# Feature-major projections in two halves of 320 tokens instead of 512 and 128

## The chip, the core and the metric

One core of one Trainium2 chip runs the kernel. The metric is the time on the device of one execution in microseconds; it is given as the median of several runs.

## What is computed

One step of a small diffusion trunk with two layers, on two groups of tokens: 512 latent tokens (x_sample, conditioned by c) and 128 context tokens (x_prompt, conditioned by c_ctx). All arithmetic is f32. Cut to what matters:

```python
D_MODEL = 1024; SEQ = 128; DEC_SEQ = 512; DEPTH = 2
H_A = H_B = H_C = 4        # three branches of 4 heads, 512 features each
N_EXPERTS = 16; D_EXPERT = 1024

h = rmsnorm(x, g_norm1) * (1.0 + sc1) + sh1          # sc1, sh1: by token group
(qa, ka, va, qb, kb, vb, zb, ab, bb, qc, kc, vc, ga, gb, gc) = split_cols(h @ w_in)
oa = diff_attention(rope(qa), rope(ka), va, ...)     # softmax(q1 k1) - lam * softmax(q2 k2)
ob = gated_head_norm(bidir_gated_delta(conv_silu(qb, kb, vb), ...), zb)
oc = neighborhood_attention(qc, kc, vc, k_ctx, v_ctx, rpb)
merged = sum(sigmoid(g_i) * (o_i @ w_br_i))
x += gate1 * (merged @ w_out)
x += gate2 * expert_choice_ffn(adaLN(rmsnorm(x)))    # 16 experts
```

Rotary positions are applied to the 512 latent tokens of qa and ka alone.

## The kernel before

**Layout.** Activations are kept feature-major: hT holds 8 groups of 128 features on the partitions and all T = 640 tokens as columns, 512 latent and then 128 context tokens. A feature-major projection (kind "fm": qb, kb, vb, zb, qa, ka, kc, qc, the gates ga and gb) loads a chunk of 1024 x 512 weights into one of three ring slots and makes 512 features, in four tiles of 128, from 8 matmuls each. "br" (w_br, 512 inputs, 4 matmuls a tile), "wo" (w_out) and "late" (the gate gc) have the same form. "tm" (va, vc) is token-major: the tokens are the weights, five units of 512 columns.

**Units.** A projection is 5 units. The first makes the 128 context columns of all four tiles into the four quarters of one PSUM bank; the others make the 512 latent columns of one tile each. Units alternate between two PSUM banks (ps). `begin(n)` lets TensorE start unit n when ScalarE has copied out unit n-2 (`unit_emptied`); `used` signals `unit_computed`.

**Order of a layer.** Program order is written out by hand on each engine.
1. Norm: VectorE scales, ScalarE shifts hT group by group (`h_ready`, L1398); TensorE's first project (L735 to L751) waits for each group k.
2. qb, kb, vb, zb by `project` (L743 context, L749 latent); ScalarE copies to `pre` (padded), VectorE convolves.
3. DeltaNet: eight L2 norms, five turns of k and v, ten groups of 128 tokens (GROUPS) of 15 dependent steps each, four output turns. After each step TensorE takes a number of quanta from a list: GAPS[gap], with STEPS = (5, 3, 2, ..., 2, 4) within a group, 5 in ("l2", j), 2 in ("kv", t), 4 in ("o", h). The list FILL holds the eight later ada chunks and folds and va, qa, kc, ka, qc, vc and the gates ga, gb. A quantum of `fill_rows` is one matmul of 512 columns (L801) or four of 128 (L792), one of `fill_tokens` (L813) is one matmul of 512. What is left of the list when the gaps are over is done before attention. ScalarE copies each unit at the gap in which it ends (DRAINS, `drain`) to one of NSTAGE = 8 stage slots of 512 columns, which lie where x was (x is spilled to memory). SP stores them (`store_plan`), waiting first for the slot of the next weight chunk (`load_plan`). The slot of unit n is used again by unit n+8.
4. Rotation: the 8 latent units of qa and ka are rotated on VectorE at hooks behind steps 7, 8, 10 and 14 of the groups, up to three of four operations a hook (a shuffle and three tensor_tensor, L1871 to L1877). GpSimd stores them one after the other (L663, `rotated_stored`).
5. Two attentions (17 query units each: one of context, then four heads of four latent tiles). SP loads K and Q when the last state is updated (L536). TensorE's loop of a unit i: scores(i+2), weigh of the finished head, late quanta, turn(i) (L1110), each of which waits for the softmax of ScalarE and VectorE. `late_units` (L829, L832) has 40 quanta: 8 at i = 0, 4 at each second and third tile of a head. ScalarE copies a late unit (L1609) behind the probabilities of the third tile.
6. Branches b, c, a, two halves each: `project` with 4 matmuls a tile; ScalarE copies a unit to `brs` (two buffers) or `brsp` (context), takes the gate's sigmoid behind the first copy (L1644), and VectorE multiplies and adds into `merged` (L2083 to L2086). After the first half-branch TensorE sums squares of oa (`sub_sums`, L1158); ScalarE takes five square roots behind the third unit of the second (L1652, L1653); VectorE scales oa head by head (`scale_sub`, L2074 reciprocal, L2075) behind four merges, SUB_AT = [(0, 1, 2), (1, 0, 0), (1, 0, 2), (1, 1, 0)] (branch, half, tile). Branch a waits for all four (`sub_scaled`).
7. wo (L1175, L1182): ScalarE scales a unit with gate1, VectorE adds it to x, then ScalarE squares and VectorE sums a feature group for the next norm.
8. The expert layer, whose 96 chunks of 2 MB a layer are loaded by SP all along.

Of the kernel before, what the change touches and what calls it, by code (L numbers as in the profile page):

```python
# [24 lines left out]
ALU = mybir.AluOpType  # L25
# [9 lines left out]
NT = T // P  # L35
NTS = TS // P
# [26 lines left out]
UNITS_OF = dict(ada=1, fm=5, tm=5, br=5, late=0)  # L63
# [44 lines left out]
XADDS = 12 + KD  # L108
# [47 lines left out]
def chunk_used(c):  # L156

    l, q = c // LAYER_CHUNKS, c % LAYER_CHUNKS
    if q < PRE_CHUNKS:
        name, i = PLAN[q]  # L160
        if kind_of(name) == "late":
            return "late_computed", 5 * (2 * l + i + 1)
        return "unit_computed", unit_no(l, name, i) + UNITS_OF[kind_of(name)]
# [47 lines left out]
NSTAGE = 8  # L211
STEPS = (5, 3, 2, 2, 2, 2, 2, 2, 2, 2, 2, 2, 2, 2, 4)
GAPS = {("l2", _j): 5 for _j in range(8)}
GAPS |= {("kv", _t): 2 for _t in range(5)}
GAPS |= {(_i, _j): _q for _i in range(10) for _j, _q in enumerate(STEPS)}
GAPS |= {("o", _h): 4 for _h in (4, 0, 1, 2, 3)}


def fill_units():

    units = []
    for name, i in FILL:
# [4 lines left out]
        else:  # L227
            units += [(name, i, j, 8) for j in range(5)]
# [23 lines left out]
ROTATED = [(_n, _j) for _n in ("qa", "ka") for _j in range(1, 5)]  # L252
# [3 lines left out]
def rotations():  # L256
# [16 lines left out]
def stage_no(name, i, j):  # L273
    return 5 * SPILLED.index((name, i)) + j
# [9 lines left out]

STAGED = [plain_stores(_d, 5 * len(SPILLED) - 1) for _d in range(NSTAGE)]


def stored(l, n):
# [3 lines left out]
    return f"stage{n % NSTAGE}_stored", 16 * (l * STAGED[n % NSTAGE] + plain_stores(n % NSTAGE, n))  # L292

# [41 lines left out]
def build(nc, A, O):  # L335
    with ExitStack() as ctx:
# [55 lines left out]
        stage = [xflat[:, 512 * i:512 * i + 512] for i in range(NSTAGE)]  # L392
        adarow = [at(7680, (512,)), xflat[:, 512 * NSTAGE:512 * NSTAGE + 512]]
# [16 lines left out]
        rot = xflat[:, 512 * (NSTAGE + 1):512 * (NSTAGE + 1) + TS]  # L410
# [4 lines left out]
        lstage = [[xflat[:, 512 * j:512 * j + 512] for j in range(5)], [at(10240 + 512 * j, (512,)) for j in range(5)]]  # L415
        gsig = [xflat[:, 0:4 * T].rearrange("p (k t) -> p k t", k=4)] + [at((17408, 12800)[i % 2], (4, T)) for i in range(5)]
        brs, brsp = at(15360, (2, TS)), at(16384, (H, TP))
        xtmp, xtmpp = at(0, (2, TS)), at(2 * TS, (H, TP))
# [34 lines left out]
        def tile_t(t):  # L453
            return slice(t * P, (t + 1) * P)

# [21 lines left out]
        def _(sp):  # L477
# [14 lines left out]
            for l in range(DEPTH):  # L492
# [15 lines left out]
                def store_plan(q):  # L508
# [4 lines left out]
                    for j in range(5):  # L513
                        n = stage_no(name, i, j)
                        if n in ROTATED_AT:
                            continue
                        sp.wait_ge(sig["unit_emptied"], unit_no(l, name, i, j) + 1)
                        if kind_of(name) == "tm":
                            dst = to[:, 512 * j:512 * j + 512]
                        elif j:  # L520
# [1696 lines left out]
```

## Time and profile before

| | us |
|---|---|
| median of 3 runs | 3558.13 (3557.75 to 3559.14) |
| the profiled execution | 3554.68 |
| its span, first to last instruction | 3552.9 |
| TensorE matmuls busy | 3376.7 (95%) |
| VectorE, ScalarE busy | 1218.2 (34%), 785.6 (22%) |

The profile has a page (shares of busy time, the span in 40 slices, DMA queues, the chain of work that ended last, groups of instructions) and a trace that is asked in views. An f32 matmul shows as two records. A record's duration is longer than the distance to the next one, because matmuls are pipelined; how fast TensorE goes is read from the distance between starts, which the chain of work adds up ("64 records, 27.47 us"). A bracket at a timeline row is the idle time ahead of it and what ended it. The clock column is TensorE's granted clock as a share of 2.4 GHz, 0.5 is 1.2 GHz. Layer 0 runs from 50 to 1750 us, layer 1 from there on.

### The profile page before, as it was taken

To read this page: it belongs to the slowest core of one execution; us is meant where nothing else is said; L and a number is where in the kernel's file an instruction comes from. 1 tells how busy PE (TensorE), PEld (TensorE's weight loads), DVE (VectorE), ACT (ScalarE), POOL (GpSimd) and SP (SyncE) were. 2 spreads that over 40 slices of the span, in tenths; PEclk is the share of its full clock that TensorE was granted. 3 is DMA by queue.
4 is the path that set the end of the run, shared out by engine and by line. 5 is a ranking of instruction groups with operands and counts; after the bars stand their busy time and mean duration, and the time that the engine had idled before them with its cause. 6 is when DMAs were issued, how large, how long until landed. Compare 5 with 4: busy or idle time off the path is not lost.

```text
span 3552.9 us, 47524 instructions
## 1 busy us (share of the span) xinstructions
PE 3376.7 (95%) x20823; PEld 1891.9 (53%) x20823; DVE 1218.2 (34%) x2250; ACT 785.6 (22%) x1695; POOL 151.9 (4%) x179
## 2 busy tenths in 40 slices
PE   7999999999999699999989999999999987999997
PEld 4557767765555244443455577677655543444444
DVE  3454443347452400000143644343563532000003
ACT  3131111125332211111122211111343321111112
POOL 1000000000100000000100000000000000000000
PEclk9999999999999899999999999999999998999999
DMA  7342332341342599999932433241532417999994
GB/s 220 98 122 72 94 93 71 94 136 60 110 162 72 204 381 393 389 395 386 369 114 71 111 88 94 67 123 39 175 98 89 153 51 285 395 389 389 394 390 163
DMA packets 217935, 675.15 MB, mean 190 GB/s; under 512 B 9786, under 2 KB 22312, under 8 KB 214144
## 3 DMA queue, kind: packets, MB, share of 16 engines
q1 hardware_dynamic: 197376, 611.35, 48.8%
q0 software_dynamic: 14640, 47.78, 5.0%
q10 hardware_dynamic: 5712, 12.99, 0.9%
q8 instruction: 164, 2.69, 0.3%
q14 instruction: 43, 0.35, 0.0%
HBM read 610.63 MB, written 66.68 MB: 191 GB/s over the span
## 4 chain that ended last, share of the span: by engine, by line
PE 90%; DVE 3%; DMA 3%; ACT 3%; issue 1%; ACTq 0%; DVEq 0%
PE unit L1257 12%; PE unit L801 12%; PE unit L749 11%; PE work L1260 9%; PE work L1257 6%; PE unit L813 4%; PE unit L792 3%; PE unit L1182 3%; PE unit L832 3%; PE unit L743 3%; PE unit L1131 2%; PE work L996 2%; PE work L1030 2%; PE unit L759 1%; PE work L1096 1%; DMA ring<-in_w_e_gate 1%
## 5 line engine op out<-in xcount | busy, mean ns | idle before, releaser
L801 PE MATMUL unit<-hT,ring 128*128 128x512 f32 x1024 | 475.5, 593 | 0.0
L1257 PE MATMUL unit<-ring,arena 128*64 128x512 f32 x1568 | 357.3, 601 | 4.3 <-DMA ring<-in_w_e_gate 2.1
L1260 PE MATMUL work<-ring,arena 128*32 128x256 f32 x4608 | 274.8, 382 | 0.0
L801 PEld LDWEIGHTS unit<-hT,ring 128*128 128x128 f32 x1024 | 177.9, 191 | 140.6 <-issue 140.6
L2167 DVE TENSOR_SCALAR arena<-work,arena 64x512 f32<-64x512 f32 x32 | 24.1, 755 | 662.5 <-PE work L1257 662.5
L1257 PEld LDWEIGHTS unit<-ring,arena 128*64 128x64 f32 x1568 | 110.7, 138 | 225.8 <-issue 219.9
L1260 PEld LDWEIGHTS work<-ring,arena 128*32 128x32 f32 x4608 | 136.8, 109 | 159.8 <-issue 80.8
L749 PE MATMUL unit<-hT,ring 128*128 128x512 f32 x512 | 221.1, 592 | 0.0
L1257 PE MATMUL work<-ring,arena 128*64 128x512 f32 x736 | 166.5, 594 | 2.1 <-ACT arena L1713 2.1
L749 PE MATMUL unit<-arena,ring 128*128 128x512 f32 x384 | 166.8, 592 | 0.0
L749 PEld LDWEIGHTS unit<-hT,ring 128*128 128x128 f32 x512 | 96.7, 190 | 118.6 <-issue 118.6
L1353 ACT ACTIVATE xT<-unit 128x512 f32<-128x512 f32 x108 | 64.4, 596 | 428.7 <-PE unit L801 318.5
L813 PE MATMUL unit<-ring,hT 128*128 128x512 f32 x320 | 146.7, 594 | 0.0
L2157 DVE TENSOR_TENSOR arena<-unit,arena 128x512 f32<-128x512 f32 x32 | 22.1, 692 | 353.9 <-PE unit L1257 353.9
L792 PE MATMUL unit<-hT,ring 128*128 128x128 f32 x1024 | 125.1, 276 | 0.0
L792 PEld LDWEIGHTS unit<-hT,ring 128*128 128x128 f32 x1024 | 119.1, 192 | 6.9 <-issue 6.9
L749 PEld LDWEIGHTS unit<-arena,ring 128*128 128x128 f32 x384 | 72.1, 190 | 86.1 <-issue 86.1
L832 PE MATMUL unit<-hT,ring 128*128 128x512 f32 x256 | 116.5, 598 | 0.0
L1182 PE MATMUL unit<-arena,ring 128*128 128x512 f32 x256 | 110.5, 592 | 0.0
L1353 ACT ACTIVATE arena<-unit 128x512 f32<-128x512 f32 x80 | 47.7, 597 | 280.7 <-PE unit L749 280.7
L1257 PE MATMUL unit<-arena 128*64 128x512 f32 x480 | 109.6, 598 | 0.0
L1257 PEld LDWEIGHTS work<-ring,arena 128*64 128x64 f32 x736 | 51.8, 137 | 103.9 <-issue 103.0
(415 smaller groups left out, 4743.6 us busy)
## 6 DMA issues: line engine op xcount, KB each, us to landing
ring<-in_w_e_gate SPq DMA_DIRECT2D x50, 2048.0 KB, 13.8
ring<-in_w_e_up SPq DMA_DIRECT2D x48, 2048.0 KB, 13.6
ring<-in_w_e_down SPq DMA_DIRECT2D x46, 2048.0 KB, 15.0
ring<-in_w_in SPq DMA_DIRECT2D x32, 2048.0 KB, 15.3
ring<-in_w_ada SPq DMA_DIRECT2D x24, 2048.0 KB, 8.9
arena<-in_w_e_down SPq DMA_DIRECT2D x18, 2048.0 KB, 14.6
arena<-in_w_e_up SPq DMA_DIRECT2D x16, 2048.0 KB, 13.1
arena<-in_w_e_gate SPq DMA_DIRECT2D x14, 2048.0 KB, 15.3
```

The lines of the kernel that those rows point to most:

```text
L743: last = mm(bank[:, tile_t(m)], w[:, k, m * P:(m + 1) * P], src[:, k, TS:T], start=k == 0, stop=k == kk - 1)
L749: last = mm(bank[:, :], w[:, k, m * P:(m + 1) * P], src[:, k, 0:TS], start=k == 0, stop=k == kk - 1)
L792: last = mm(bank[:, tile_t(m)], w[:, k, m * P:(m + 1) * P], hT[:, k, TS:T], start=k == 0, stop=k == KD - 1)
L801: last = mm(bank[:, :], w[:, k, m * P:(m + 1) * P], hT[:, k, 0:TS], start=k == 0, stop=k == KD - 1)
L813: last = mm(big[:, :], hT[:, k, tile_t(t)], w[:, k, :], start=k == 0, stop=k == KD - 1)
L832: last = mm(ps[1][:, :], w[:, s, (j - 1) * P:j * P], hT[:, s, 0:TS], start=s == 0, stop=s == KD - 1)
L996: last = mm(W[(3, 1, 3)[s]][:, tile_t(h)], gD4[:, h, :], (gX if s else gP)[:, h, :], start=True, stop=True)
L1030: last = mm(W[(1, 0, 1)[s]][:, tile_t(h)], gZT[:, h, :], (gV if s else gV0)[:, h, :], start=True, stop=True)
L1182: last = mm(bank[:, :], w[:, k, m * P:(m + 1) * P], merged[:, k, 0:TS], start=k == 0, stop=k == KD - 1)
L1257: last = mm(big[SLS * c:SLS * c + SLS, :], x, w[:, kk, 512 * c:512 * c + 512], start=k == 0, stop=k == KD - 1)
L1260: last = mm(low[SLOTP * c:SLOTP * c + SLOTP, 0:256], xp, w[:, kk, 256 * c:256 * c + 256], start=k == 0, stop=k == KD - 1)
L1353: emptied(a_(dst, unit(n)[:, :], f))
```

## The change

All 640 tokens of a feature-major projection are taken as two halves of HT = 320 columns, so the second half holds 192 latent and the 128 context columns. A projection is then 8 units of 320 columns (fm: tile by tile, both halves; br and wo: all tiles of the first half, then of the second). Token-major units stay at 5 of 512.

- Fill: fill_rows has 64 quanta of one matmul of 320 columns. GAPS becomes 8 for l2, 3 for kv, STEPS = (8, 5, 3, ..., 3, 6), 6 for o.
- Staging: 10 stage slots of 320 columns for fm, 2 of 512 for tm; SP stores all units but two of a chunk before it waits to load the next one, and the last two behind.
- Rotation: 16 pieces (320 or 192 columns), up to four operations a hook.
- Late: 8 units, 8 quanta at each second and third tile of a head; a copy behind the probabilities at both.
- Branches: merges in halves; gates' sigmoid behind unit 0; the square roots behind unit 3 of the second half-branch; SUB_AT applies at the second half of its tile (unit 4 + tile).
- wo: units of one tile and one half; residual and squares follow; x is added in 16 pieces.

```diff
-UNITS_OF = dict(ada=1, fm=5, tm=5, br=5, late=0)
+UNITS_OF = dict(ada=1, fm=8, tm=5, br=8, late=0)
+NLATE = 8
...
-NSTAGE = 8
-STEPS = (5, 3, 2, 2, 2, 2, 2, 2, 2, 2, 2, 2, 2, 2, 4)
-GAPS = {("l2", _j): 5 for _j in range(8)}
-GAPS |= {("kv", _t): 2 for _t in range(5)}
+NSTAGE = 10
+NROWSTAGE = 2
+STEPS = (8, 5, 3, 3, 3, 3, 3, 3, 3, 3, 3, 3, 3, 3, 6)
+GAPS = {("l2", _j): 8 for _j in range(8)}
+GAPS |= {("kv", _t): 3 for _t in range(5)}
...
-GAPS |= {("o", _h): 4 for _h in (4, 0, 1, 2, 3)}
+GAPS |= {("o", _h): 6 for _h in (4, 0, 1, 2, 3)}
...
-ROTATED = [(_n, _j) for _n in ("qa", "ka") for _j in range(1, 5)]
+ROTATED = [(_n, _j) for _n in ("qa", "ka") for _j in range(8)]
...
-        n = min(3, 4 * len(ready) - at)
+        n = min(4, 4 * len(ready) - at)
...
                 for q in range(8, last + 3):
+                    store_plan(q - 3, False)
                     load_plan(q)
-                    store_plan(q - 3)
+                    store_plan(q - 3, True)
...
             def project(l, name, i, src, kk=KD, wait=None):
-                for m in range(4):
+                for u in range(8):
+                    m, f = (u % 4, u // 4) if kind_of(name) == "br" else (u // 2, u % 2)
+                    bank = begin(unit_no(l, name, i, u))
                     for k in range(kk):
-                        if wait and m == 0:
+                        if wait and u == 0:
                             pe.wait_ge(*wait(k))
-                        last = mm(bank[:, tile_t(m)], w[:, k, m * P:(m + 1) * P], src[:, k, TS:T],
-                                  start=k == 0, stop=k == kk - 1)
-                used(last)
-                for m in range(4):
-                    bank = begin(unit_no(l, name, i, 1 + m))
-                    for k in range(kk):
-                        last = mm(bank[:, :], w[:, k, m * P:(m + 1) * P], src[:, k, 0:TS],
+                        last = mm(bank[:, 0:HT], w[:, k, m * P:(m + 1) * P], src[:, k, half_t(f)],
                                   start=k == 0, stop=k == kk - 1)
                     used(last)
...
                         if i and AUNITS[i][1] in (1, 2):
                             if AUNITS[i][1] == 1:
                                 pe.wait_ge(sig["attn_out"], NPV * nb + AUNITS[i][0] + 1)
-                            for _ in range(KD // 2):
-                                next(extra)
+                            for _ in range(KD):
+                                next(extra, None)
...
-                        if i and AUNITS[i][1] == 2:
-                            copy_late(1 + AUNITS[i][0])
+                        late = 2 * AUNITS[i][0] + AUNITS[i][1]
+                        if i and AUNITS[i][1] in (1, 2) and late < NLATE:
+                            copy_late(late)
...
+                        for u in range(8):
+                            at_ = 8 * (6 * l + g) + u
+                            if at_ >= 2:
+                                act.wait_ge(sig["merged_ready"], at_ - 1)
+                            copy_unit(unit_no(l, "br" + s, half, u), brs[:, u % 2, :], words=HT)
+                            if u == 0:
+                                act.wait_ge(sig[f"gate{half}_loaded"], 16 * (3 * l + b + 1))
+                                a_(gsig[g], gsig[g], ACT.Sigmoid).then_inc(sig["gate_ready"], 1)
+                            if g == 1 and u == 3:
...
+                            merge(merged[:, 4 * half + m, half_t(f)], gsig[2 * b + half][:, m, half_t(f)], brs[:, u % 2, :])
+                            if f and (b, half, m) in SUB_AT:
                                 scale_sub(SUB_AT.index((b, half, m)))
```

## Rows read from the trace of the kernel before

**Rows 1.** The page: busy us with share and count; the granted clock in 40 slices.
```profile
PE 3376.7 (95%) x20823; PEld 1891.9 (53%) x20823; DVE 1218.2 (34%) x2250; ACT 785.6 (22%) x1695; POOL 151.9 (4%) x179
PEclk9999999999999899999999999999999998999999
```

**Rows 2.** Stretches: length; busy of PE, PEld, DVE, ACT, POOL; clock; DMA; GB/s.
```profile
300.00:600.00 300.00, 300.00 (x1741) 212.37 (x1740) 130.84 (x256) 47.99 (x110) 3.77 (x7) 1.00 0.35 92
...
975.00:1155.00 180.00, 178.90 (x661) 99.63 (x660) 65.33 (x75) 54.15 (x73) 0.00 (x0) 1.00 0.32 116
```

**Rows 3.** The chain of work that ended last: start, length, records.
```profile
59.21 27.47 PE unit L749 x64
86.68 7.14 PE unit L743 x64
```

**Rows 4.** Timeline, TensorE, matmuls of two columns: start, length.
```profile
34.89 1.05 PE L770 MATMUL work<-cst,arena 128*128 128x2 f32 x8
```

**Rows 5.** Grouped view, 128-column records: first and last of five: busy, mean ns, idle.
```profile
L792 PE MATMUL unit<-hT,ring 128*128 128x128 f32 x1024 | 125.1, 276 | 0.0
...
L1175 PE MATMUL unit<-arena,ring 128*128 128x128 f32 x256 | 29.2, 275 | 0.0
```

**Rows 6.** Timeline, TensorE and VectorE, end of the DeltaNet stage, layer 0.
```profile
763.37 1.88 PE L801 MATMUL unit<-hT,ring 128*128 128x512 f32 x4
...
769.48 7.03 PE L801 MATMUL unit<-hT,ring 128*128 128x512 f32 x16
779.09 0.65 PE L1053 MATMUL work<-cst,arena 128*128 128x128 f32 x4 [2.57 <-DVE arena L1962]
...
769.68 1.12 DVE L1946 SCALAR_TENSOR_TENSOR arena<-arena,sc,work 128x128 f32<-128x128 f32 x4 [2.82 <-PE work L1042]
...
775.93 3.10 DVE L1962 TENSOR_TENSOR arena<-arena,sc 128x512 f32<-128x512 f32 x5
...
791.23 0.63 PE L1068 MATMUL work<-cst,arena 128*128 128x128 f32 x4 [1.15 <-ACT xT L1353]
```

**Rows 7.** Timeline, TensorE, last head of the first attention, layer 0.
```profile
875.11 3.60 PE L832 MATMUL unit<-hT,ring 128*128 128x512 f32 x8
...
880.22 0.66 PE L1110 MATMUL unit<-cst,arena 128*128 128x128 f32 x4 [1.08 <-DVE arena L2053]
```

**Rows 8.** Branch stage: timeline of ScalarE and VectorE, then groups for the widths.
```profile
1008.90 1.28 ACT L1652 ACT_TABLE_LOAD   x1
1010.20 2.42 ACT L1652 ACTIVATE arena<-work,cst 128x512 f32<-128x512 f32 x4
...
1042.28 4.15 DVE L2074 RECIPROCAL arena<-arena 128x640 f32<-128x640 f32 x1
1046.46 0.89 DVE L2075 SCALAR_TENSOR_TENSOR arena<-arena,vcol 128x640 f32<-128x640 f32 x1
...
L2158 DVE TENSOR_TENSOR arena<-work,arena 128x256 f32<-128x256 f32 x32 | 13.3, 414 | 0.0
...
L2086 DVE TENSOR_TENSOR arena<-arena 128x512 f32<-128x512 f32 x40 | 27.7, 692 | 1.4
...
L1713 ACT ACTIVATE arena<-work 128x256 f32<-128x256 f32 x32 | 12.1, 379 | 0.0
...
L1353 ACT ACTIVATE arena<-unit 128x512 f32<-128x512 f32 x80 | 47.7, 597 | 280.7 <-PE unit L749 280.7
```

**Rows 9.** Stretches behind two lulls of TensorE, columns as in rows 2.
```profile
200.00:204.00 4.00, 4.00 (x16) 1.08 (x18) 1.38 (x1) 1.92 (x3) 0.00 (x0) 0.50 0.03 11
...
1795.00:1800.00 5.00, 3.40 (x9) 2.25 (x10) 5.00 (x11) 5.00 (x11) 0.00 (x0) 0.50 0.15 50
```

**Rows 10.** TensorE's waits (total, times, longest), and the chain at layer 1's start.
```profile
PE unit L743 <- ACT hT L1398: 7.1, 1, 7.1
...
1794.99 7.50 ACT hT L1398 x16
```

**Rows 11.** GpSimd's stores of the rotated units (L663), from issue to landing.
```profile
DMA to landing us min/median/max: 2.3/2.3/11.7
```

More of the change, by code:

```diff
@@ L227, in fill_units @@
         else:
-            units += [(name, i, j, 8) for j in range(5)]
+            units += [(name, i, j, KD) for j in range(UNITS_OF[kind_of(name)])]
     return units
@@ L282, in plain_stores, with row_stores @@
     return sum(n not in ROTATED_AT for n in range(d, last + 1, NSTAGE))
-STAGED = [plain_stores(_d, 5 * len(SPILLED) - 1) for _d in range(NSTAGE)]
+def row_stores(d, last):
+    return len(range(d, last + 1, NROWSTAGE))
+STAGED = [plain_stores(_d, 8 * len(COL_SPILLED) - 1) for _d in range(NSTAGE)]
+ROWSTAGED = [row_stores(_d, 5 * len(ROW_SPILLED) - 1) for _d in range(NROWSTAGE)]
 def stored(l, n):
@@ L391, in build @@
         xflat = xT.rearrange("p k t -> p (k t)")
-        stage = [xflat[:, 512 * i:512 * i + 512] for i in range(NSTAGE)]
-        adarow = [at(7680, (512,)), xflat[:, 512 * NSTAGE:512 * NSTAGE + 512]]
+        stage = [xflat[:, HT * i:HT * i + HT] for i in range(NSTAGE)]
+        rowstage = [xflat[:, HT * NSTAGE + 512 * i:HT * NSTAGE + 512 * i + 512] for i in range(NROWSTAGE)]
+        behind = HT * NSTAGE + 512 * NROWSTAGE
+        adarow = [at(7680, (512,)), xflat[:, behind:behind + 512]]
         (gE, gL, gAT, gD, gDT, gI, gD2, gD2T, gD4, gP, gX, c32, gN, gVB, gKB, gKD) = [
@@ L533, in spilled @@
                     sp.wait_ge(sig["rotated_stored"], 16 * (l * len(ROTATED) + r))
+                    last = 5 * sum(f in ROW_SPILLED for f in before) - 1
+                    for d in range(NROWSTAGE):
+                        sp.wait_ge(sig[f"rowstage{d}_stored"], 16 * (l * ROWSTAGED[d] + row_stores(d, last)))
                 def back(dst, name, i, done):
@@ L818, in late_units @@
             def late_units(l, i):
-                for j in range(5):
-                    n = 5 * (2 * l + i) + j
+                for j in range(NLATE):
+                    n = NLATE * (2 * l + i) + j
                     w = chunk_in(chunk_no(l, *LATE[i]))
@@ L1350, in copy_context, with copy_unit @@
                 emptied(a_(dst, h4(unit(n)), f))
[L1352 to L1353 removed]
+            def copy_unit(n, dst, f=ACT.Copy, words=512):
+                emptied(a_(dst, unit(n)[:, 0:words], f))
             def ada(l, a):
@@ L2107, in _ @@
                 dve.wait_ge(sig["x_moved"], 16 * (2 * l + 2))
                 for half in range(2):
-                    add_x(unit_no(l, "wo", half), half)
+                    for u in range(8):
+                        m, f = u % 4, u // 4
+                        dve.wait_ge(sig["unit_emptied"], unit_no(l, "wo", half, u) + 1)
+                        x = xT[:, 4 * half + m, half_t(f)]
+                        TT(x, x, xtmp[:, u % 2, :], ALU.add).then_inc(sig["x_added"], 1)
+                        if f:
+                            add_square(2 * l + 1, 4 * half + m)
```

231 lines of the change are left out of this document (102 added, 129 removed).

## The prediction

> **What bounds the kernel now.** I read the page's shares and clock first: TensorE is busy 3376.7 of 3552.9 us at nearly the full clock, so it is the bound unless a stage says otherwise [rows 1]. The table of stretches says where: in the DeltaNet stage (300 to 600 us) it is busy 300 of 300 us, and in the branch and output projections (975 to 1155) 178.9 of 180 [rows 2]. Two things therefore count: the time that TensorE's own matmuls take, and each place where the change takes away work that now covers a wait.
>
> A trace record is one pass; an f32 matmul has two. In the chain, 64 records of 512 columns take 27.47 us and 64 of 128 columns take 7.14 [rows 3]. So the **pitch** is 429.2 ns at 512 columns and 111.6 at 128. One projection unit of the kernel before (16 records) is 6.87 us, its 128-column unit (64 records) 7.14 us, and a whole projection 34.6 us.
>
> **Part 1, the halves themselves.** Each pair of a 512- and a 128-column record (540.8 ns) becomes two of 320. There are 1024+512+384+256+256 = 2432 such pairs, in five groups of the grouped view; its first and last stand in [rows 5]. No 320-column record is in the trace. Eight records of 2 columns last 1.05 us together, the last one about 0.27, so their pitch is 0.111 us too [rows 4]: at 128 columns the pitch is the weights' load, not the columns. 1024 column-cycles at 2.4 GHz are 426.7 ns, so a 512-column record has 2.5 ns on top; a 320-column one by the same account takes 266.7+2.5 = 269.2 ns. Bounds: in proportion 268.3, on the line between the two pitches 270.4. I take 269.2, since it rests on the longer record, in which the columns are the limit. 2432 x (540.8 - 538.4) = **-5.8 us** (bounds -10 and 0). The Trainium skill ("TensorE: Matmul & The Clock Gate", section on the extra 2.5 ns) gives a fixed 2.5 ns for every matmul whatever its width. That rule by itself would make the halves worth nothing, as there are as many matmuls as before; the trace's 111.6 at both 2 and 128 columns speaks for a small gain.
>
> A layer starts with TensorE waiting for hT: in layer 1 7.1 us for the first group, and then ScalarE delivers eight groups in 7.5 us, one every 0.94 [rows 10]. TensorE fills these waits with two records of 128 columns per group now and two of 320 then, so it has more done when the last group comes; the clock is at its lower level there [rows 9]. Layer 0 gains next to nothing (there most groups are ready when the weights land), layer 1 some 2.5: **-2.7 us**. The last unit's copy in front of the L2 norms and the last one of wo are shorter: 0.2 us each, twice per layer, **-0.8 us**.
>
> **Part 2, the fill of the DeltaNet stage.** Between its dependent steps TensorE takes "quanta" from a list. Before: 424 quanta for 430 slots of GAPS, so the list ends in the gap after the third output turn. After: 24 for ada and fold, 80 for va and vc, 8 x 64 = 512 for the rest, 616 in all. The slots become 64+15+550+30 = 659. va and vc keep their 512-column quanta but are now taken three at a time where two were taken, so the list runs dry early: 574 slots lie ahead of group 9, 42 quanta are left for its 55 slots, and they end in its gap 11. Empty are gaps 12, 13 and 14 of group 9 and all five "o" gaps. Everywhere else a gap of 3 x 0.538 = 1.62 us stands for 2 x 0.858 = 1.72 (four records 763.37 to 765.09) [rows 6]. VectorE's answer in such a gap takes 0.2 + 0.69 us, so some 0.7 us of slack stays and the narrower gap costs nothing.
>
> Now the end of the stage in layer 0 [rows 6]. From L1042's end at 769.48 VectorE needs until 775.93 + 3.10 = 779.03 for the normed output, 9.55 us. Before, 16 records (6.87 us) covered it and TensorE waited 2.57. After, nothing covers it: +6.9. Gaps 12 and 13 become waits of 0.9 us each: +1.8. Of the four output turns each waits for VectorE's two scalings (1.1 us), before hidden but for 1.15 us at 791.23: 0.7 + 0.4 + 1.5 after, +1.4. Together **+10.0 us a layer, +20.0**. The K and Q loads that attention needs start with the last state update, then about 13 us ahead of attention; I take them as hidden; uncovered they would add at most some 3 us a layer.
>
> **Clock.** TensorE then stands nearly idle for some 15 us. The trace has its clock at 1.2 GHz after each lull: 0.50 at 200 to 204, though busy 4.00 of 4.00, and 0.50 at 1795 to 1800 [rows 9]. So I expect the turns, the key turns and the first 3 to 6 us of attention at half speed: +3.5 us a layer, bounds 0 and +7. With a smaller lull at the end of the first attention (+1): **+9 us**.
>
> **Part 3, attention with the late projection.** Before: 40 quanta, 8 at the start and 4 in each of eight slots. After: 64, 8 at the start and 8 (4.31 us) in the first seven slots; the eighth, in the last head, is empty. The work is the same, its cover is not. The last slot holds 8 records (3.43 us) at 875.11, and TensorE still waits 1.08 us behind it for VectorE [rows 7]. In the first attention all 3.4 us turn to waiting, plus 0.4 for a copy (ScalarE, 320 columns) that now stands in front of the last exponentials: +3.9. The second has shorter exponentials, so about 1.5 of it, plus 0.25 at each second slot of a head, where TensorE now waits until ScalarE has emptied the bank: +2.6. The copies (0.43 where it was 0.60) in front of exponentials that TensorE waits for give back 0.17 seven times: -1.2. **+5.3 us a layer, +10.6** (bounds 0 and 8 a layer).
>
> **Part 4, branch projections.** Units are now 8 of 2.15 us (8 records), where they were 3.57 and four of 3.43; buffers are two in PSUM and two in SBUF either way. So TensorE may run ahead of a blocked ScalarE or VectorE by less time. Widths: VectorE 0.41 at 256 and 0.69 at 512 columns, so 0.48 at 320 and 1.0 for a merge of two operations; ScalarE 0.38 at 256 and 0.60 at 512, so 0.43 at 320 [rows 8]. I went through the units one by one with these. (a) First half-branch: the sigmoid (1.28 table + 2.34) now sits between the copies of units 0 and 1: 0.7 us. (b) The square roots for the sub-norm, 1.28 + 2.42 + 0.6 = 4.3 us on ScalarE [rows 8], now cover two units of 2.15 instead of two of 3.43: 1.1 us. (c) scale_sub is 4.15 + 0.89 = 5.0 us on VectorE [rows 8], four times; two pairs of them stand 4.3 us apart (before 6.9), each between merges of 1.0 us per 2.15. VectorE falls behind, and units 3 of half-branches 2 and 3 wait 0.4 and 2.4. (d) The fourth scale_sub comes after unit 4, at 10.8 us of its half-branch, where it came at 7.0; branch a waits for it: 0.3. Sum 4.9, **+5.0 us a layer, +10.0** (bounds 3 and 7).
>
> Staging: 8 stores instead of 5 a projection, more DMAs issued by SP, the first six ahead of the next weights' load; these loads have a whole chunk's time (34.6 us and more), so nothing. Rotation: 64 pieces instead of 32 but at 0.4 to 0.5 us instead of 0.7, about the same VectorE time per hook, with slack. wo: TensorE waits once for the first halves of the merges and once for all, each with four units of 4.31 us in hand: nothing.
>
> **Sum.** -5.8 - 2.7 - 0.8 + 20.0 + 9 + 10.6 + 10.0 = +40.3 us. The profiled execution took 3554.7 us (span 3552.9 and 1.8 around it), 3.4 below the median of the runs; 3554.7 + 40.3 + 3.4 = **3598 us**.
>
> **Rivals.**
> (A) Milder: the lull does not lower the clock long and attention's and the branches' waits are half of mine: 3598 - 9 - 10 = 3579. For it: VectorE and ScalarE are far from full over these stretches. 18%.
> (B) Staging bites: the tenth stage slot comes round after ten units of 320 columns. In group 1, kc unit 6 needs the slot of qa unit 4, rotated one hook before, and ka unit 1 that of qa unit 7. GpSimd's stores land in 2.3 us, but 11.7 when weights are under way [rows 11]. ScalarE is held in drain then, and behind it the copy for which the next merge waits. One or two such waits of 5 us a layer: 3598 + 16 = 3614. Against: the second slot is needed about 12 us after its store. 12%.
> (C) Faster: the stage is bound by the chain, not by TensorE. A record's duration exceeds its pitch (1.05 us for eight at 0.111) [rows 4], so holes below 0.16 us a gap could hide in "busy". Then the third quantum of va and vc would go into holes, and the early end of the list would cost nothing. It decides if a two-quanta gap is longer than 1.72 us. Then part 2 turns from +20 to -20 and its 7 us of clock vanish: 3598 - 47 = 3551. Against: 763.37 to 765.09 is just four pitches. 4%.
> (D) No change, the parts cancel or the late waits vanish in TensorE's slack elsewhere: 3558. 6%. By the skill's rule on width (part 1) alone the sum would be 3604; that is inside the forecast.
>
> **Chances.** Forecast (3585 to 3608) 60%, A 18, B 12, C 4, D 6. 0.2% (7 us) is about what a measurement of this kernel can tell from no change. Faster 5%, same 6%, slower 89%. The range takes in A and B, leaves out C and D and the ends: 3571 to 3616.
>
> **What would show it.** Records of 320 columns at a pitch of 269 ns; the fill's last record in gap 11 of group 9, then a wait of 9.5 us for L1962's counterpart and the clock at 1.2 GHz after it; a wait of some 4 us for the last probabilities in each layer's first attention; waits of TensorE on unit copies between 975 and 1060, the longest in the fourth half-branch. I am wrong if the fill's gaps show waits in the middle of the stage, if the pitch is off by over 2 ns, or if attention's empty slot costs nothing.

## The result, and the profile after

The changed kernel takes 3595.05 us (median of four runs, 3593.64 to 3597.39) beside 3558.07 us for the kernel before: ratio 1.0104, 95% interval 1.0088 to 1.012. It is slower by 1%, and 3598 was predicted (3571 to 3616). The medians are 37.0 us apart. The profiled execution took 3594.47 us, its span is 3592.7; between the last starts of TensorE in the two profiled executions there are 40.2 us, and the comparison by stages below goes by these.

The page answers to [rows 1]: as many matmuls, 7 us more busy, and the wait is elsewhere.

```profile
PE 3383.8 (94%) x20823; PEld 2089.6 (58%) x20823; DVE 1238.7 (34%) x2402; ACT 809.9 (23%) x1855; POOL 161.1 (4%) x195
PEclk9999999999999899999999999999999998999998
```

**The pitch.** Two rows of the chain of work that ended last (start, length, records), first a projection between two others, then wo. They answer to [rows 3].

```profile
156.04 34.66 PE unit L771 x128
...
1102.04 68.92 PE unit L1184 x256
```

256 records of 320 columns in 68.92 us are 269.2 ns each, the predicted number. (128 in 34.66 are 270.8, with the unit waits of that stretch in it.) The Trainium skill has a fixed 2.5 ns per matmul at 2.4 GHz ("TensorE: Matmul & The Clock Gate", section "Wait — 56ns, not 53.3ns?"); with the column times of part 1 the trace agrees at 320 and 512 columns: 266.7 + 2.5 and 426.7 + 2.5. At the old 128-column records the same account would be 106.7 + 2.5 = 109.2 and the trace has 111.6; these 2.4 ns a pair are the whole gain in pitch, 5.8 us over the 2432 pairs.

**The end of the fill.** TensorE's timeline in layer 0: start, length, what, records, and in brackets the idle time ahead and what ended it. It answers to [rows 6].

```profile
776.13 1.24 PE L814 MATMUL unit<-hT,ring 128*128 128x320 f32 x4
...
779.04 1.16 PE L1037 MATMUL work<-arena 128*128 128x128 f32 x8 [0.78 <-DVE arena L1949]
780.98 1.16 PE L1047 MATMUL work<-arena 128*128 128x128 f32 x8 [0.78 <-DVE arena L1949]
781.97 1.06 PE L1049 MATMUL work<-arena 128*128 128x128 f32 x8
792.47 1.11 PE L1060 MATMUL work<-cst,arena 128*128 128x128 f32 x4 [9.44 <-DVE arena L1972]
```

The last two quanta (four records) lie in gap 11 of group 9. The two gaps behind it are waits of 0.78 us, and then TensorE stands for 9.44 us where it stood 2.57. The first output turn lasts 1.11 us instead of 0.65: the clock is down.

**The clock.** Stretches of the changed kernel; columns as in rows 2, the granted clock is the last but two.

```profile
786.00:795.00 9.00, 2.50 (x11) 2.10 (x12) 4.48 (x9) 4.06 (x9) 0.00 (x0) 0.50 0.95 342
796.00:802.00 6.00, 3.45 (x35) 2.88 (x36) 3.25 (x10) 1.29 (x3) 1.21 (x3) 1.00 1.09 413
2555.00:2564.00 9.00, 4.79 (x20) 3.85 (x20) 7.09 (x14) 0.88 (x1) 0.00 (x0) 0.50 1.02 343
2564.00:2570.00 6.00, 4.67 (x28) 4.20 (x30) 1.54 (x7) 1.29 (x3) 2.80 (x4) 0.50 1.04 412
888.00:898.00 10.00, 6.99 (x14) 3.76 (x15) 2.34 (x8) 1.63 (x3) 0.00 (x0) 0.50 0.28 100
2752.00:2758.00 6.00, 5.22 (x11) 2.66 (x10) 0.00 (x0) 1.19 (x2) 0.00 (x0) 0.50 0.43 161
```

The same lull of 9.4 us stands in both layers. In layer 0 TensorE is back at 2.4 GHz when attention begins (798 us); in layer 1 it stays at 1.2 GHz for 6 us of it. The last two rows are further places: the end of the first attention in layer 0 and that of the second in layer 1.

**The end of the first attention**, layer 0, TensorE's timeline; it answers to [rows 7].

```profile
884.35 0.60 PE L1117 MATMUL unit<-cst,arena 128*128 128x128 f32 x4
885.73 0.63 PE L1117 MATMUL unit<-cst,arena 128*128 128x128 f32 x4 [0.78 <-ACT arena L1603]
890.23 1.11 PE L1117 MATMUL unit<-cst,arena 128*128 128x128 f32 x4 [3.87 <-DVE arena L2063]
...
892.97 7.09 PE L1138 MATMUL unit<-arena 128*128 128x512 f32 x10 [0.78 <-ACT arena L1606]
```

The empty slot lies between 884.35 and 885.73. The wait of 3.87 us for the last probabilities (1.08 before) is the predicted one in place and near it in size: with the wait of 0.78 ahead of it, which was not there before, 3.6 us are added, for a term of +3.9. What follows was priced at 1 us: the weigh of ten records lasts 7.09 us, where ten at full clock last 4.5, and from the start of the last turn to the weigh it is 2.74 us (890.23 to 892.97) for 1.93.

**The branch stage**, the chain in layer 0. The view keeps the longest pieces, so short ones are missing between the rows; work of DVE and ACT in the chain stands for waits of TensorE.

```profile
1020.73 1.28 ACT L1663
1022.61 1.83 ACT arena L1663 x3
1025.40 6.74 PE unit L771 x24
1032.68 1.28 ACT L1659
1034.34 1.88 issue
1036.69 4.59 PE unit L771 x16
1042.85 4.08 DVE arena L2084
1046.95 0.88 DVE arena L2085
1049.69 4.07 DVE arena L2084
1053.79 0.89 DVE arena L2085
1056.12 4.59 PE unit L771 x16
```

TensorE's starts show five waits in front of units: 0.38 us (until 996, behind the first sigmoid), 1.08 (1025, behind the roots), 0.42 (1036), 2.10 (1056, behind the second pair of scalings) and 0.32 (1067, for the last scaling). Predicted were 0.7, 1.1, 0.4, 2.4 and 0.3. The third stands where it was predicted and has the predicted size, but the chain shows another cause: not a scaling on VectorE but ScalarE's next table load (L1659, 1.28 us at 1032.68) with its sigmoid.

**The stages.** How much longer a stage takes on TensorE than before, from the first start of each stage (us; before starts at 199.10, 791.23, 887.36, 975.85 and 1153.35 in layer 0). The kernels behind "after" are those of the experiments; the changed kernel's +40.2 is the sum of its column. Each column is one execution: that of e1 was the fastest of its five (3566.87 us, median 3575.86), that of e3 the slowest of its four (3603.11, median 3597.14).

| layer, stage | after | e1 | b1 | e2 | e3 | e4 | d1 | e6 |
|---|---|---|---|---|---|---|---|---|
| 0, start to L2 norms | -2.5 | -2.7 | -0.4 | -0.8 | -0.9 | -0.7 | -1.6 | -0.5 |
| 0, DeltaNet with output turns | +9.4 | -1.0 | +9.4 | +9.7 | +9.6 | +9.8 | +9.4 | -0.9 |
| 0, first attention | +6.5 | +6.7 | +1.4 | +6.8 | +6.1 | -0.2 | +5.0 | -0.3 |
| 0, second attention | 0.0 | 0.0 | -1.7 | 0.0 | +6.7 | -1.5 | +5.7 | -1.5 |
| 0, branches and wo | +4.0 | +4.0 | 0.0 | +0.2 | +4.0 | +5.7 | +4.0 | +0.2 |
| experts of layer 0, 1 to L2 norms | -3.6 | -5.1 | +1.4 | -3.1 | -3.0 | -3.5 | -5.3 | -4.8 |
| 1, DeltaNet with output turns | +8.4 | -1.6 | +9.0 | +8.3 | +8.4 | +8.3 | +10.1 | +2.3 |
| 1, first attention | +8.8 | +6.6 | +1.6 | +8.7 | +5.7 | +1.9 | +7.7 | +1.3 |
| 1, second attention | +5.5 | +1.7 | 0.0 | +5.4 | +7.9 | +0.5 | +5.7 | +0.1 |
| 1, branches and wo | +4.1 | +4.1 | 0.0 | +0.2 | +4.1 | +4.1 | +4.1 | +0.2 |
| rest | -0.4 | 0.0 | +1.4 | -1.4 | +0.3 | +0.8 | -1.8 | -1.8 |
| all | +40.2 | +12.6 | +22.2 | +34.1 | +48.9 | +25.0 | +43.0 | -5.6 |

The sixth row mixes two things. Split at the first sum of squares of layer 1's norm (1785.78 us before), the way from there to the L2 norms is 3.9 us shorter in the changed kernel and 3.8 to 4.1 shorter in every other kernel of 320 columns, where b1 and b2, the old form, have +0.7 and +1.5. That gain is the change's own.

### The profile page after: what moved, and what is told of

Its sections match the earlier page's. It is cut to its first block, busy times and chain, and to the rows that moved or that the text cites. A ratio compares the mean times of both kernels' runs of the same rounds, so it can differ in the third digit from the quotient of the medians.

```text
span 3592.7 us, 48060 instructions
## 1 busy us (share of the span) xinstructions
PE 3383.8 (94%) x20823; PEld 2089.6 (58%) x20823; DVE 1238.7 (34%) x2402; ACT 809.9 (23%) x1855; POOL 161.1 (4%) x195
## 4 chain that ended last, share of the span: by engine, by line
PE 87%; DVE 5%; DMA 4%; ACT 3%; issue 1%; POOL 0%; ACTq 0%; DVEq 0%
PE unit L814 15%; PE unit L1259 12%; PE unit L771 12%; PE work L1262 9%; PE work L1259 6%; PE unit L826 4%; PE unit L1184 4%; PE unit L839 3%; PE unit L1138 2%; DMA ring<-in_w_e_gate 2%; PE work L1037 2%; PE work L1003 1%; PE unit L781 1%; PE work L1103 1%; PE unit L1117 1%
## 5 line engine op out<-in xcount | busy, mean ns | idle before, releaser
L814 PE MATMUL unit<-hT,ring 128*128 128x320 f32 x2048 | 600.1, 434 | 0.0
L814 PEld LDWEIGHTS unit<-hT,ring 128*128 128x128 f32 x2048 | 367.6, 191 | 126.8 <-issue 10.4
L771 PE MATMUL unit<-hT,ring 128*128 128x320 f32 x1024 | 281.0, 438 | 13.2 <-ACT hT L1400 7.2
L771 PEld LDWEIGHTS unit<-hT,ring 128*128 128x128 f32 x1024 | 197.0, 193 | 95.7 <-issue 9.6
L771 PE MATMUL unit<-arena,ring 128*128 128x320 f32 x768 | 210.3, 434 | 8.4 <-ACT arena L1355 6.7
L771 PEld LDWEIGHTS unit<-arena,ring 128*128 128x128 f32 x768 | 145.0, 190 | 73.5 <-ACT arena L1355 10.7
L1355 ACT ACTIVATE xT<-unit 128x320 f32<-128x320 f32 (+1 forms) x156 | 72.5, 465 | 435.5 <-PE unit L814 376.7
L839 PE MATMUL unit<-hT,ring 128*128 128x320 f32 x512 | 145.2, 437 | 0.1
L1184 PE MATMUL unit<-arena,ring 128*128 128x320 f32 x512 | 138.1, 432 | 0.0
L839 PEld LDWEIGHTS unit<-hT,ring 128*128 128x128 f32 x512 | 95.6, 190 | 47.0 <-issue 8.3
L1184 PEld LDWEIGHTS unit<-arena,ring 128*128 128x128 f32 x512 | 97.4, 190 | 40.4
L1355 ACT ACTIVATE arena<-unit 128x320 f32<-128x320 f32 x136 | 59.1, 437 | 271.1 <-PE unit L771 249.6
```

The costliest lines, as they stand in the source:

```text
L771: last = mm(bank[:, 0:HT], w[:, k, m * P:(m + 1) * P], src[:, k, half_t(f)], start=k == 0, stop=k == kk - 1)
L814: last = mm(bank[:, 0:HT], w[:, k, tile_t(u // 2)], hT[:, k, half_t(u % 2)], start=k == 0, stop=k == KD - 1)
L839: last = mm(ps[1][:, 0:HT], w[:, k, tile_t(j // 2)], hT[:, k, half_t(j % 2)], start=k == 0, stop=k == KD - 1)
L1184: last = mm(bank[:, 0:HT], w[:, k, m * P:(m + 1) * P], merged[:, k, half_t(f)], start=k == 0, stop=k == KD - 1)
L1355: emptied(a_(dst, unit(n)[:, 0:words], f))
```

## The experiments

The theory is that of the prediction: the halves themselves gain a little, and three places lose cover (the early end of the list, the empty late slot, blocks of 4 to 5 us on ScalarE and VectorE between short units), each with a low clock where TensorE stood. The rivals are that the 320-column form costs by itself, or that the stage is bound by its chain. Each ratio is against the kernel before as it ran beside that experiment (medians 3555.3 to 3556.0 us, where it was 3558.07 beside the changed kernel), so the difference between medians of two experiments is good to some 2 us.

### e1: the list dealt out by time

```diff
-STEPS = (8, 5, 3, 3, 3, 3, 3, 3, 3, 3, 3, 3, 3, 3, 6)
-GAPS = {("l2", _j): 8 for _j in range(8)}
...
+STEPS = (5, 3, 2, 2, 2, 2, 2, 2, 2, 2, 2, 2, 2, 2, 4)
+WIDE = {("l2", _j): 5 for _j in range(8)}
...
+        cost += dict(ada=[0.86] * 2, fold=[0.4], tm=[0.858] * 40).get(kind, [0.538] * 64)
...
+    for gap, n in WIDE.items():
+        due += 0.858 * n * SCALE
+        k = 0
+        while at < len(cost) and done + cost[at] / 2 <= due:
+            done += cost[at]
+            at += 1
+            k += 1
+        out[gap] = k
...
+SCALE = 0.985
+GAPS = gaps()
```

> The changed kernel with one thing else: the quanta of each gap of the DeltaNet stage are dealt out by time (0.538 us for a quantum of 320 columns, 0.858 for one of 512) against the time that the gap had before (5, 3, 2 ... 2, 4 quanta of 0.858 us). There are 616 slots for 616 quanta, and the last quanta lie in the last output gap. Theory (the loss is the list's early end): the wait for the normed output (L1972's counterpart) goes from 9.4 back to about 2.6 us, no stretch at 1.2 GHz between the end of the stage and the first attention in either layer, the stage with its turns 9.4 and 8.4 us shorter and layer 1's first attention some 2 more: -20 us against the changed kernel, 3575 (3570 to 3579). Rival (the stage is bound by its chain, and narrow gaps cost as much as the empty ones): 3590 to 3597, the wait short but other waits in the middle of the stage.

Measured 3575.86 us (ratio 1.0058, 1.0044 to 1.0072). The stage goes from +9.4 and +8.4 to -1.0 and -1.6 us. At its end there are matmuls of 320 columns between all output turns, and the wait for the normed output is 2.98 us ([rows 6] have 2.57):

```profile
773.19 0.66 PE L1082 MATMUL work<-cst,arena 128*128 128x128 f32 x4 [2.98 <-DVE arena L1994]
...
787.50 0.66 PE L1097 MATMUL work<-cst,arena 128*128 128x128 f32 x4 [0.59 <-ACT xT L1377]
```

So the 320-column gaps are no worse than the old ones, and 20 us of the loss (+17.8 to -2.6 in the stage) were the sizes of the gaps in a table. The first attention keeps its +6.7 and +6.6 with nothing low ahead of it: that loss is its own. In layer 1 the second attention loses 3.8 us less: here its last weigh is at full clock, where in the changed kernel the ten records take 6.72 us, and its first head is 0.9 us shorter. Why the clock fell there in the one kernel and not in the other, no run shows.

### b1: the old kernel with an early end

```diff
-GAPS = {("l2", _j): 5 for _j in range(8)}
+GAPS = {("l2", _j): 8 - (_j == 7) for _j in range(8)}
```

> The kernel before, its projections in 512 and 128, with one thing of the change alone: seven of the eight gaps of the L2 norms take 8 quanta and the last one 7, where all took 5, so that the list runs dry in gap 11 of group 9, as it does in the changed kernel. Theory: the same loss as there, 8.5 to 10 us a layer in the stage and its turns and 1 to 4 us a layer from the clock at 1.2 GHz behind it: 3558 + 22 = 3580 (3575 to 3587). Rival (the loss belongs to the 320-column form, not to the empty gaps): 3558, within 3 us.

Measured 3575.72 us (1.0057, 1.0043 to 1.0071). The old kernel now shows the same wait to the hundredth, in the place where [rows 6] have 2.57:

```profile
794.43 1.11 PE L1053 MATMUL work<-cst,arena 128*128 128x128 f32 x4 [9.44 <-DVE arena L1962]
```

+9.4 and +9.0 in the stage, and +1.4 and +1.6 in the first attention, in which nothing else was changed: the granted clock is at 0.5 for another 3.4 us from 802.2 and from 2563.4. The early end costs the same in the old form: it has nothing to do with 320 columns.

### e2: the sub-norm's work spread

```diff
-SUB_AT = [(0, 1, 2), (1, 0, 0), (1, 0, 2), (1, 1, 0)]
+SUB_AT = [(0, 1, 2), (0, 1, 4), (0, 1, 6), (1, 0, 1), (1, 0, 3), (1, 0, 6), (1, 1, 0), (1, 1, 3)]
...
-                            if g == 1 and u == 3:
+                            if g == 1 and u in (1, 2, 3, 4):
...
-                    ch.link(v_.reciprocal(rt1[:, h, :], rt1[:, h, :]))
+                    r, o = rt1[:, h, half_t(f)], oaT[:, h, half_t(f)]
+                    ch.link(v_.reciprocal(r, r))
```

> The changed kernel with the sub-norm's work spread: the square roots one head behind each of the units 1 to 4 of the second half-branch, where all stand behind unit 3, and the scaling of oa in eight pieces of 320 columns behind eight merges, where four whole heads stand behind four. The work is the same. Theory (ScalarE's 4.3 us and VectorE's 5.0 us blocks outlast the two buffers of 2.15 us units): the waits of 1.1, 0.4, 2.1 and 0.3 us in front of units go, the first one (0.4, behind the sigmoid) stays; -3.6 us a layer, -7 in all, 3588 (3586 to 3590). Rival (short units cost TensorE by their number, at every copy and merge): the stage keeps its length, 3594 to 3596.

Measured 3589.17 us (1.0094, 1.0079 to 1.011). The stage goes from +4.0 and +4.1 to +0.2 us, the theory's -3.6 to 0.3 us. In its chain the roots and the scalings are gone (two rows of layer 0):

```profile
1013.91 19.40 PE unit L771 x72
...
1037.86 62.71 PE unit L771 x232
```

Three of the four waits that were to go are gone. The one of 0.42 us stays in both layers. ScalarE's and TensorE's timelines in layer 0 name its cause, the table load and the sigmoid between the copies of two units:

```profile
1033.85 1.28 ACT L1659 ACT_TABLE_LOAD   x1
1035.14 2.34 ACT L1659 ACTIVATE arena<-arena 128x2560 f32<-128x2560 f32 x1
...
1037.86 1.34 PE L771 MATMUL unit<-arena,ring 128*128 128x320 f32 x4 [0.25 <-ACT arena L1355]
```

### e3: the empty slot at the front

```diff
-                        if i and AUNITS[i][1] in (1, 2):
+                        if i and AUNITS[i][1] in (1, 2) and i > 2:
...
-                        late = 2 * AUNITS[i][0] + AUNITS[i][1]
+                        late = 2 * AUNITS[i][0] + AUNITS[i][1] - 1
```

> The changed kernel with the empty late slot of each attention at the front: no quanta at the second tile of the first head, and units 1 to 7 one slot later each, the last one in the last head. Theory (the empty slot costs what the answer to it needs at that place, and at the end of the stage a low clock besides): at the front 4.3 us of matmuls leave a wait of 2.3, at the end 4.3 us of matmuls take the place of a wait of 3.9; with the last weigh back at full clock -4 us in each layer's first attention, and -0 to -3 in layer 1's second, where the bias of the second head comes late: 3585 (3582 to 3589). Rival (the empty slot costs the same wherever it lies): 3592 to 3596.

Measured 3597.14 us (1.0114, 1.0099 to 1.013): the theory's number is missed by 12 us. The end of the first attention does as expected (the last wait of 3.87 is 0.78, the weigh at full clock). But the front costs two waits, where one of 2.3 was expected:

```profile
816.48 0.66 PE L1117 MATMUL unit<-cst,arena 128*128 128x128 f32 x4 [2.54 <-DVE arena L2063]
...
820.51 0.66 PE L1117 MATMUL unit<-cst,arena 128*128 128x128 f32 x4 [2.09 <-DVE arena L2063]
```

and the second attention loses 6.7 and 2.4 us more. In layer 0, 4.1 of the 6.7 lie in the last head, where 4.3 us of matmuls now stand in place of a wait of 1.3. The first head is 1.5 us longer although it has 4.3 us of matmuls less, and the second 1.1. The chain names why: the bias table of the second head, behind GpSimd's five stores that clear moe_sum.

```profile
901.76 2.64 POOL moe_sum L705 x5
...
905.25 18.08 DMA arena<-rpb_scratch
```

With the front empty TensorE comes to the second head before this load has landed (no run has the empty front with the stores moved). What follows for the theory: not "a slot lost is a wait of 3.9", but a distance. From the turn of one tile to the turn of the tile after the next, ScalarE copies and exponentiates and VectorE combines, 5.9 us (884.35 to 890.23 in the fence of the changed kernel's end); a wait comes where TensorE has less than that between these two turns. The first head has a short weigh (1.2 us) ahead of its second tile, so an empty slot there is short twice.

### e4: the empty slot one place earlier in the last head

```diff
-                        if i and AUNITS[i][1] in (1, 2):
-                            if AUNITS[i][1] == 1:
+                        if i and AUNITS[i][1] in (1, 2) and i != NA - 3:
+                            if AUNITS[i][1] == 1 or i == NA - 2:
```

> The changed kernel with one late unit moved by one slot: the last unit lies at the third tile of the last head, and the second tile of that head is the empty slot. Theory (the place decides: in the records of the kernel with the empty slot at the front, TensorE's turn of a tile needs ScalarE and VectorE for some 5.6 us after the turn of two tiles before; between two such turns TensorE has its scores, a weigh or a late unit; with the second tile of a later head empty there is always one weigh or one unit of 4.3 us in between, with the third tile empty there is none): the wait of 3.9 to 4.1 us for the last probabilities goes to about 1, the weigh behind it is back at full clock, -6 us in each first attention, -1 to -3 in each second: 3594 - 16 = 3578 (3574 to 3583). Rival (an empty slot costs the same wherever it lies, as the one at the front did): 3591 to 3597.

Measured 3580.33 us (1.0073, 1.0058 to 1.0088), 15 us less than the changed kernel (13 if each is taken against the kernel before beside it), for a unit moved by one slot. The first attention goes from +6.5 to -0.2 and from +8.8 to +1.9 (layer 1 has the low clock from the fill's lull ahead of it), the second one from 0.0 to -1.5 and +5.5 to +0.5. The end in layer 0:

```profile
882.47 0.66 PE L1117 MATMUL unit<-cst,arena 128*128 128x128 f32 x4
882.97 4.47 PE L839 MATMUL unit<-hT,ring 128*128 128x320 f32 x16
887.28 0.60 PE L1117 MATMUL unit<-cst,arena 128*128 128x128 f32 x4
889.08 0.66 PE L1117 MATMUL unit<-cst,arena 128*128 128x128 f32 x4 [1.20 <-DVE arena L2063]
...
891.00 4.53 PE L1138 MATMUL unit<-arena 128*128 128x512 f32 x10 [0.83 <-ACT arena L1606]
```

The turn at 882.47, in front of the unit, has no wait at all, though its slot is empty. The place decides, as this theory said. (The +5.7 in layer 0's branches is the +4.1 of the other layer and a dip of the clock to 0.84 between 1045 and 1056 us that layer 1 doesn't have.)

### d1: work in the empty slot

```diff
+                        if i == NA - 2:
+                            pe.wait_ge(sig["late_emptied"], NLATE * (nb + 1))
+                            for k in range(KD):
+                                mm(ps[1][:, 0:HT], hT[:, k, tile_t(0)], hT[:, k, half_t(1)], start=k == 0, stop=k == KD - 1)
                         turn(i)
```

> The changed kernel with eight more matmuls of 320 columns (4.3 us, their result is not used) in the empty slot, the third tile of the last head, of each of the four attentions: 17.2 us of added work on TensorE. Theory (TensorE stands waiting there, and its clock falls for that): in the first attentions the wait of 4.1 becomes about 0.5 and the weigh behind it is back at full clock, -2 to -3 us each; in the second ones the wait is 1.6, so the work costs some 2.7 us less what the clock gives back: in all 3594 - 5 + 3 = 3592 (3587 to 3597). Rival (the slot is no idle time of TensorE but time that it spends anyway): +17 us, 3611.

Measured 3601.17 us (1.0135, 1.012 to 1.015), between the two and 4 us above the theory's range. In the first attentions 4.3 us of added matmuls make the stage 1.5 and 1.0 us shorter (+5.0 and +7.7 instead of +6.5 and +8.8): the wait was idle time and the low clock came from it. In the second attentions the same work costs 5.7 and 0.2 us. The theory had 2.7 less what the clock gives back for these. In layer 0 there is no low clock to give back; TensorE waits 1.0 us more, for the bank that the added work needs, and 1.3 less for the probabilities, so the last head is 4.0 us longer. The other 1.6 us lie in the first head, where this execution has a low clock (0.57 from 902 to 906) that the changed kernel has not. The profiled execution is 3.0 us above that of the changed kernel, the medians 6 and the ratios 0.0031, which is 11 us: 17.2 us of work for 3 to 11 us.

### e5, e6, e7: the mends together; b2: mends in the old kernel

e5 is e1, e2 and e4 in one. e6 has this besides, and e7 is e6 again, run beside b2:

```diff
                     if h == 1:
                         pool.wait_ge(sig["pv_computed"], NPV * (2 * l + 1))
-                        for t in range(NT):
-                            pool.dma_start(moesum[l][tile_t(t), :], ...).then_inc(sig["scattered"], 16)
...
                             .then_inc(sig[f"bias{h % 2}_loaded"], 16)
+                    if h == 3:
+                        for t in range(NT):
+                            pool.dma_start(moesum[l][tile_t(t), :], ...).then_inc(sig["scattered"], 16)
```

b2 is the kernel before with that edit and e2's.

> Three of the mended parts together: gaps dealt out by time, the sub-norm's work spread, and the empty late slot at the second tile of the last head. Theory (the three losses are separate and add): measured were -27.6 us of span for the gaps and -7.6 for the spread; with -6.6 in each first attention and -1.5 in all in the second ones (the rest went with the gaps' clock) the span is 3592.7 - 27.6 - 7.6 - 14.7 = 3543, some 10 us under the kernel before: ratio 0.997 (0.9955 to 0.9985). Rival (the halves themselves cost TensorE something that the three parts only cover): not below the kernel before, ratio 1.000 to 1.003.

> The same with one more edit: GpSimd issues the five 512 KB stores that clear moe_sum behind the bias loads of the last head, where it issues them ahead of the load for the second head, so that this load does not lie behind them (18 to 19 us from issue to landing, 6 without them in front). Theory: the bias of the second head is in time in both layers; the second attention of layer 1 gains the 1.4 us that TensorE waited for it and perhaps a low clock behind it, layer 0 nothing to 1 us: 1 to 4 us under the kernel with three parts. Rival (the load was in time but for one wait that other work hides): the same time within 1 us.

> The kernel with all four mends once more, beside the old kernel with two of them: the gaps by time, the sub-norm's work spread, the empty late slot at the second tile of the last head, the bias loads first. Theory (what is left is the pitch of 269.2 ns against half of 540.8 and the earlier start of a layer, 6 to 12 us in all): ratio 0.9965 to 0.9985. Rival (it was the scatter of the runs): 0.999 to 1.001.

> The kernel before, projections in 512 and 128, with two of the mends: square roots one head behind each latent unit of the second half-branch and oa scaled in eight pieces of 320 columns, and the stores that clear moe_sum behind the last bias loads. Theory (the mends remove only waits that the 320-column form made): the kernel before has none of these waits, so it stays as it is: ratio 1.000, within 0.0015. Rival (they are worth as much in the old form, and the halves themselves gain nothing): -7 to -10 us, ratio 0.997 to 0.998.

| kernel | median, us | ratio to before | 95% |
|---|---|---|---|
| e5 | 3550.51 | 0.9980 | 0.9968 to 0.9992 |
| e6 | 3548.68 | 0.9976 | 0.9968 to 0.9985 |
| e7 (e6 again) | 3547.40 | 0.9981 | 0.9962 to 1.0001 |
| b2 | 3556.13 | 1.0003 | 0.9994 to 1.0012 |

With the mends the halves are 5 to 8 us faster than the kernel before by medians, 0.2%; the interval of e7 just includes no change. The old kernel gains nothing from two of them. The other two were not tried in it, so what is shown is that these halves beat the kernel before as it stands, not that no 512 and 128 form could be as fast. The three parts of e5 do not add up to the forecast span of 3543: the profiled one is 3549.2. The 27.6 us for the gaps came from the fastest execution of e1, and e5's has a low clock at the end of layer 0's DeltaNet stage (0.54 from 776 to 783), where the stage is +2.8 and the first attention +1.3. By medians the parts would give 3595.05 - 19.2 - 5.9 - 14.7 = 3555.3, and e5 took 3550.51. e6's own edit is worth 0.6 us on TensorE in layer 1's second attention (+0.7 in e5, +0.1 in e6), not the 1.4 expected. Two rows of the waits, of e5 and of e6, of that attention (total, times, longest):

```profile
DVE arena L2050 <- POOL arena L738: 5.6, 1, 5.6
```

```profile
POOL arena L739 <- DMA arena<-rpb_scratch: 14.6, 3, 9.1
```

In e5 VectorE waits 5.6 us for the bias; in e6 that wait is gone and GpSimd's longest wait for a load is 9.1 us instead of 18.2. But e4's slot had already left TensorE only 0.8 us of waits for probabilities there. The edit goes the right way and is below what the times can tell.

## Why the prediction was right

Predicted +40.3 us, measured +40.2 between TensorE's last starts in the profiled executions and +37.0 by medians. By stage, both layers (a layer's way to the L2 norms taken from its norm on, the experts with the rest):

| | predicted | measured |
|---|---|---|
| to the L2 norms (pitch 1.2, start 2.7, copies 0.4) | -4.3 | -6.5 |
| DeltaNet and both attentions (20.0 + 9 + 10.6 - pitch 3.1) | +36.5 | +38.6 |
| branches and wo (10.0 - pitch 1.5 - copies 0.4) | +8.1 | +8.1 |
| rest | 0 | +0.1 |

- **Part 1** stands: 269.2 ns. The gain at a layer's start came too (-2.5 and -3.9 us). Layer 1's is within 0.3 us the same in all kernels of 320 columns, for 3.3 predicted; layer 0's moves by 2 us from kernel to kernel (the first row of the table of stages), so it is not resolved.
- **The fill's end** stands in place and size: gap 11 of group 9, 9.44 us for 9.5, 0.78 for 0.9. With the turns at the low clock the stage is +9.4 and +8.4; e1 takes it away and b1 makes it anew. Rival C (bound by the chain) falls with them.
- **The clock** was right as a term and wrong in its places. I had put 3.5 us a layer behind the fill, 7 in all. The stage with its turns came out at +17.8 where I had 17.5 without any clock, and attention behind it lost 0 in layer 0 and 2.1 in layer 1 (+8.8 against e1's +6.6): 2.4 of the 7. Behind the empty slot I had 1 us a layer, 2 in all. It was 3.4 and 3.2 in the first attentions (weighs of 7.09 and 6.88 us for 4.53, and 0.8 more in the turns ahead of each) and 2.9 in layer 1's second one (6.72 for 4.53, and 0.7 ahead of it): 9.5. The clock cost 11.9 us in all, where 9 was predicted.
- **Attention's late slot**: the waits added in the first are 3.6 for 3.9. The second slot costs 1.7 us for 2.6: e1 has +1.7 in layer 1, without a low clock and a late load. In layer 0 the changed kernel shows 0.0 only because the kernel before lost 1.7 us at that attention's start to its own low clock (0.83 in the stretch 888 to 898), which b1 and b2 do not have. The copies gave back less: each of the middle heads of the first attention is 1.6 us longer, by its 1.74 us of added matmuls less 0.15, where 0.17 was to come back at each copy. In layer 1 the second attention also lost 0.9 us in its first head for the late bias load, which the prediction did not name. Without the clock, that load and the kernel before's own low clock, 10.0 us are left for the two attentions of both layers, as predicted (10.6 less 0.6 of pitch).
- **The closeness of the total** is luck in part. The clock cost 2.9 us more than predicted and the late load 0.9; the kernel before's low clock took off 1.7 and the layers' starts 2.2 more than predicted. The mechanism of each part stands without that; the agreement to 0.1 us does not.
- **The branches** stand in place and, taken together, in size: 4.3 us of waits a layer, and 0.1 at each restart behind them, less 0.8 of pitch, are the +4.0. e2 leaves two of the five waits, and the same account gives its +0.2. One cause was wrong: the wait of 0.4 us in the third half-branch was put down to VectorE's scalings and is ScalarE's table load and sigmoid. That its size came out is luck, since the first sigmoid, with the same work, was put at 0.7 and cost 0.38.
- **Rival B** (staging holds ScalarE): its waits for transfers are 5.7 us once, for g_final, and twice 0.9 at the end; none for a stage slot. **Rival A** (half the waits) falls in the branches and in attention. By the Trainium skill's fixed 2.5 ns at every width, part 1 would be nothing and the sum +46. The total could not have told the two apart, the pitch does: the old 128-column records take 111.6 ns, not 109.2.

## What to carry to other kernels

When filler work is cut in other sizes, deal it out by time and look where the list ends: a surplus taken early is missing at the end, where the longest wait stands. When a loop has one filler unit less than slots, leave empty the slot whose neighbours still cover the answer; here one slot decided 15 us. Blocks on the helping engines (a reciprocal of 4.1 us, roots of 4.3) must be shorter than the buffered units ahead of them, so smaller units mean splitting the blocks.

## What the hardware showed besides

- In a wait of 3.9 us of TensorE the clock falls to 1.2 GHz in both layers (0.50 from 888 to 898) and stays there, although weigh and turns fill most of that stretch; a wait of 1.2 us (e4) leaves it at 1.00. But the waits of 0.78 and 1.33 us at the end of the second attention of the changed kernel are followed by 0.50 in layer 1 (2752 to 2758) and by full clock in layer 0. So the length of the one wait does not decide it. Two equal lulls of 9.44 us cost different amounts behind them, since the clock was back at 796 us in layer 0 and only after 2570 in layer 1.
- Repeats of one program differ, and their clock with them. The twelve runs of e5 go from 3539.4 us at a mean granted clock of 0.983 to 3561.0 at 0.977, with the same code. A difference of a few us between two single executions is read from the stages, not from the spans.
- Two DMAs of 240 KB that read the bias table take 18 us (e3, layer 0) behind five stores of 512 KB issued by the same engine, and GpSimd waits at most 9.1 us for any load of it in layer 1's second attention when the stores are issued later (e6), where it waited up to 18.2 (e5).
